# Opening in three sweeps, modulation loads one block later, six stage joints moved ahead, a candidates' search without copies, experts opened by quarters

## The chip, the core and the metric

The kernel runs on one core of one Trainium2 chip. The metric is device time in microseconds (us) of one execution; three runs give a median. The core's engines run side by side and wait for one another through semaphores: PE (TensorE, matmuls into the banks of `ps`), ACT (ScalarE), DVE (VectorE), and SP (SyncE), which here only issues DMAs, all of them on one queue in the order of the program.

## What is computed

Two transformer blocks on 256 tokens of width 2048. Cut to what the change touches:

```python
h = rms_norm(x, ln_gain); z = h @ w_in + b_in              # first projection: 77 blocks of 128 columns
y_a, y_b, y_c = recurrent(z), sparse_attention(z), decayed_attention(z)   # with silu gates
merged = sum(sigmoid(z_merge[j]) * (y_j @ w_branch[j]) for j in range(3))
h = x + merged @ w_out
h = h + sigmoid(h @ w_ple_gate) * rms_norm(p @ w_ple, ple_gain)
mod = silu(c) @ w_mod + b_mod                              # 96 blocks of modulation rows, on VectorE
h1, hc = modulate(h), modulate(ctx)                        # tokens and context, 256 rows each
# second mixer: projections of both (y), of the tokens alone (l), two branches, merge, w_out
q = modulate(h2) @ peer_w_q
s = einsum(q, sub_keys)                                    # 32 rows of 128 scores per token
top_s, top_i = top_k(s, 16)                                # "top"
best = top_k(top_s[0] + top_s[1], 16); wts = softmax(best) # "cand"
weights[expert, t] = wts spread over the 128 x 128 experts # "expw"
y = (weights * gelu(u @ h2)) .T @ v                        # 16384 experts, in 32 groups of 512
out = rmsnorm(h2 + g2 * y)
```

## The kernel before

Everything is transposed: a tile holds 128 channels by 256 tokens, 16 such tiles make one activation (`DC = 16`, `T = 256`). A weight block is 1 MB (128 columns of 2048 rows) or 0.5 MB, loaded into one of four slots of `ring` (`SLOTS = 4`); the load into a slot waits on SP until `weights_used` says that the block four before has been multiplied. Most products are made in three parts to keep precision: ACT rounds the weights (`round_z`, `round_block`, `round_branch`, ...), DVE subtracts to get the remainder (`split_z`, `split_block`, ...), and PE makes rounded x rounded, rounded x remainder and remainder x rounded, 48 matmuls for a 1 MB block (`three_products`, `split_products`). Rounding runs two blocks ahead of PE. The three engines' programs are written out by hand, stage behind stage; each engine executes its own strictly in order, so the order of calls in `n1_act`, `n1_dve`, `merge_act`, `out_act`, `experts_act` and so on sets what waits for what. ACT takes a finished block out of its bank with `keep_gate` or a copy.

Places that the change and the prediction speak of, in order of the program:

- **Opening** (`n1_*`). SP loads x in four quarters, then `consts` (848 KB) and `params` (294 KB), the first block of w_z, `cond` (2 MB), `misc`, `p`, and the first blocks of w_mod between those of w_z. ACT squares x; PE sums the squares with a matrix of ones from `consts` (16 float32 matmuls, L856); ACT takes the root, DVE inverts it and scales x by it; ACT rounds quarter after quarter (`r0` to `r3`, L832), DVE makes their remainders (`l0` to `l3`), and PE starts the first block when `l0` is there.
- **Modulation chunks** (`mod_chunk`, L760 and L763): 52 of the 96 are made by DVE inside the first projection's loop, ahead of the split of the block two further on; a chunk is one or two multiplications with accumulation over 2048 columns. `load_mod` on SP waits until the chunk two before is used.
- **Six joints** between stages, in which the next stage's first weights are rounded and split only after the last block of the stage before has been taken out: gates to branch products (`merge_*`), branch products to the ple product and w_out (`out_*`), ple gate to y (`n2_*`), y to l, second gates to second branch products (`merge2_*`), and those to the second w_out (`round_last`, `split_last`).
- **Candidates** (`choose_*`). DVE makes eight rounds of `top`, each of four score rows, then four rounds of `cand`; ACT makes the exponentials of a round of `cand`. Meanwhile PE multiplies the first four expert groups (`early`, 64 matmuls a group), and ACT applies the gelu to each. PE then needs `cand` and all four gelus to transpose the mixing weights (`mix`).
- **Expert weights** (`expw_*`): 64 rounds in a loop; for each DVE makes one block-diagonal tile (L3319) and two one-hot tiles (L3323), PE spreads them, ACT copies them out.
- **Experts** (`experts_*`): ACT rounds the normed activation in quarters, DVE makes remainders, then both go over the first 16 pieces of u; DVE clears the sum `yacc` (L3589), and the v phases begin.

## Time and profile before

| | |
|---|---|
| median of three runs | 4459.39 us (4456.03 to 4464.69) |
| the profiled execution's own time | 4466.13 us |
| its span, first to last instruction | 4464.4 us |
| mean granted clock of TensorE | 0.972 |
| data moved by DMA | 764.42 MB, mean 171 GB/s |
| PE, DVE, ACT busy | 95%, 67%, 45% of the span |

A row of a timeline gives the start and length in us of an instruction (or of several alike, xN), and in brackets how long its engine had been idle before it and what ended that. A granted clock of 1.0 stands for 2.4 GHz, 0.5 for 1.2 GHz.

### The profile page before, as it was taken

The page shows a single profiled execution, that of the slowest core. Times are in us where ns is not written, and L with a number is a line of the kernel's source. Part 1 is how long each engine was busy: PE and PEld are TensorE (multiplying, and loading weights), DVE is VectorE, ACT ScalarE, POOL GpSimd, SP SyncE. Part 2 cuts the span into 40 slices and gives each one's busy share as a digit, 9 for nine tenths or more (in the row PEclk, how much of TensorE's full clock was granted, in tenths as well). Part 3 has the DMA queues.
Part 4 walks back from the last instruction along what each step waited for, and adds up shares of the span by engine and source line. Part 5 has one row for each costly group of instructions (what it writes and reads, how often), then busy time and mean ns, then how long its engine had stood idle before and what let it go on. Part 6 is the DMA issues. An engine that isn't in the chain of part 4 may idle for free.

```text
span 4464.4 us, 66743 instructions
## 1 busy us (share of the span) xinstructions
PE 4220.8 (95%) x27552; PEld 3763.9 (84%) x27552; DVE 3004.3 (67%) x4776; ACT 2016.0 (45%) x3194; POOL 0.2 (0%) x4
## 2 busy tenths in 40 slices
PE   7999889999999989979998999988999999999998
PEld 7999868998988886778886999988788888888886
DVE  7887754666767664457776554687776767666666
ACT  4444464444452242444443434156455555555554
POOL 0000000000000000000000000000000000000000
PEclk9999999999999999989998999999999999999999
DMA  7888533367755442200002554424555454555552
GB/s 283 319 314 309 176 129 129 123 230 272 276 186 189 171 151 78 99 22 1 1 1 76 162 205 153 172 95 203 212 195 220 185 216 190 211 195 206 200 201 95
DMA packets 136927, 764.42 MB, mean 171 GB/s; under 512 B 12352, under 2 KB 30016, under 8 KB 67392
## 3 DMA queue, kind: packets, MB, share of 16 engines
q1 hardware_dynamic: 136640, 760.32, 46.5%
q8 instruction: 213, 3.49, 0.3%
q14 instruction: 74, 0.61, 0.0%
HBM read 737.20 MB, written 23.07 MB: 170 GB/s over the span
## 4 chain that ended last, share of the span: by engine, by line
PE 70%; DVE 9%; ACT 3%; DMA 2%; issue 1%; DVEq 0%; SPq 0%; ACTq 0%
PE ps L3450 15%; PE ps L3421 9%; PE ps L917 6%; PE ps L919 6%; PE ps L918 6%; PE ps L3423 5%; PE ps L2789 1%; PE ps L3349 1%; PE ps L2792 1%; PE ps L846 1%; PE ps L3341 1%; PE ps L847 1%; PE ps L848 1%; PE ps L2780 1%; DMA ring<-w_branch_dram 1%
## 5 line engine op out<-in xcount | busy, mean ns | idle before, releaser
L3450 PE MATMUL ps<-pieces,gact_parts 128*128 128x512 f32 x3072 | 710.5, 392 | 13.5 <-DVE pieces L3545 7.7
L3450 PEld LDWEIGHTS ps<-pieces,gact_parts 128*128 128x128 f32 x3072 | 578.9, 189 | 137.4 <-issue 6.6
L3421 PE MATMUL ps<-hp_parts,pieces 128*128 128x512 f32 x1792 | 635.6, 399 | 7.7 <-DVE pieces L3545 7.7
L848 PE MATMUL ps<-x_rounded,ring_rounded 128*128 128x256 f32 x2000 | 563.3, 282 | 0.0
L3545 DVE TENSOR_TENSOR pieces<-ring,pieces 128x512 fp32r<-128x512 f32 x464 | 320.8, 692 | 272.8 <-ACT pieces L3488 272.4
L3423 PE MATMUL ps<-hp_parts,pieces 128*128 128x256 f32 x1792 | 503.8, 281 | 0.0
L3488 ACT ACTIVATE pieces<-ring 128x512 fp32r<-128x512 f32 x464 | 293.0, 632 | 354.6 <-PE ps L3423 265.2
L3488 ACT ACTIVATE pieces<-area 128x512 fp32r<-128x512 f32 x496 | 311.6, 630 | 312.3 <-PE ps L3450 201.5
L3545 DVE TENSOR_TENSOR pieces<-area,pieces 128x512 fp32r<-128x512 f32 x496 | 341.4, 690 | 160.6 <-ACT pieces L3488 152.2
L3421 PEld LDWEIGHTS ps<-hp_parts,pieces 128*128 128x128 f32 x1792 | 337.6, 188 | 91.6 <-issue 7.9
L848 PEld LDWEIGHTS ps<-x_rounded,ring_rounded 128*128 128x128 f32 x2000 | 379.9, 190 | 0.0
L846 PE MATMUL ps<-x_rounded,z_rounded 128*128 128x256 f32 x1232 | 347.7, 282 | 17.2 <-DVE ring_rounded L814 10.4
L847 PE MATMUL ps<-hn_rest,z_rounded 128*128 128x256 f32 x1232 | 346.9, 282 | 0.0
L3423 PEld LDWEIGHTS ps<-hp_parts,pieces 128*128 128x128 f32 x1792 | 339.3, 189 | 1.1
L909 DVE TENSOR_TENSOR ring_rounded<-ring,ring_rounded 128x1024 fp32r<-128x1024 f32 x168 | 197.9, 1222 | 198.9 <-ACT ring_rounded L904 198.9
L919 PE MATMUL ps<-x_rounded,ring_rounded 128*128 128x256 f32 x1088 | 310.2, 285 | 0.0
L917 PE MATMUL ps<-x_rounded,ring_rounded 128*128 128x256 f32 x832 | 245.0, 294 | 21.9 <-DVE ring_rounded L909 21.9
L846 PEld LDWEIGHTS ps<-x_rounded,z_rounded 128*128 128x128 f32 x1232 | 233.2, 189 | 18.3 <-DVE ring_rounded L814 10.0
L846 PE MATMUL ps<-x_rounded,ring_rounded 128*128 128x256 f32 x768 | 224.0, 292 | 19.8 <-DVE ring_rounded L1008 19.5
L918 PE MATMUL ps<-hcat_rest,ring_rounded 128*128 128x256 f32 x832 | 238.7, 287 | 0.0
L814 DVE TENSOR_TENSOR ring_rounded<-ring,z_rounded 128x1024 fp32r<-128x1024 f32 x154 | 181.6, 1222 | 77.9 <-ACT z_rounded L808 77.6
L847 PEld LDWEIGHTS ps<-hn_rest,z_rounded 128*128 128x128 f32 x1232 | 233.3, 189 | 0.0
(538 smaller groups left out, 9425.7 us busy)
## 6 DMA issues: line engine op xcount, KB each, us to landing
ring<-u_dram SPq DMA_DIRECT2D x128, 1024.0 KB, 6.4
area<-v_dram SPq DMA_DIRECT2D x124, 1024.0 KB, 8.9
ring<-w_mod_dram SPq DMA_DIRECT2D x96, 1024.0 KB, 7.0
ring<-w_mg_dram SPq DMA_DIRECT2D x80, 1024.0 KB, 4.9
ring<-w_z_dram SPq DMA_DIRECT2D x77, 1024.0 KB, 6.9
ring<-w_branch_dram SPq DMA_DIRECT2D x80, 512.0 KB, 4.2
ring<-w_out_dram SPq DMA_DIRECT2D x32, 1024.0 KB, 5.0
ring<-w_y_dram SPq DMA_DIRECT2D x20, 1024.0 KB, 4.8
```

Source lines behind the costliest of these rows:

```text
L846: nc.tensor.matmul(out, rounded, hn_rounded[:, k, :], start=first, stop=False)
L847: nc.tensor.matmul(out, rounded, hn_rest[:, k, :], start=False, stop=False)
L848: return nc.tensor.matmul(out, rest, hn_rounded[:, k, :], start=False, stop=last)
L909: nc.vector.tensor_tensor(rest_piece(at, q), raw_piece(at, q), buffer(piece + q).bitcast(F32), ALU.subtract).then_inc(weights_split, 1)
L917: nc.tensor.matmul(out, w, rounded, start=(k == 0), stop=False)
L918: nc.tensor.matmul(out, w, rest, start=False, stop=False)
L919: return nc.tensor.matmul(out, w_rest, rounded, start=False, stop=(k == DC - 1))
L3421: both = nc.tensor.matmul(bank(s).rearrange("p (a t) -> p a t", t=T), piece[:, b, 0, k * P:(k + 1) * P], hp2[:, :, c, :], start=(c == 0), ...
L3423: last = nc.tensor.matmul(bank(s, 0, T), piece[:, b, 1, k * P:(k + 1) * P], hp2[:, 0, c, :], start=False, stop=(c == DC - 1))
L3450: last = nc.tensor.matmul(out, gact[:, k, ga, s, t * P:(t + 1) * P], piece[:, b, va, :], start=(s == 0 and w == 0), stop=(s == GROUP - 1 a ...
L3488: nc.scalar.activation(piece[:, n % NPIECES, 0, :], source, ACT.Copy).then_inc(rounded, 1)
L3545: nc.vector.tensor_tensor(piece[:, b, 1, :], source, piece[:, b, 0, :].bitcast(F32), ALU.subtract).then_inc(remainders, 1)
```

## The change

1. The opening: the ones are made in the kernel by a memset, pairs of squares are added on DVE so that PE sums 8 matmuls instead of 16, ACT loads the root's table first, and the first three blocks are multiplied in three sweeps: rounded by rounded for all three, then rounded by the activation's remainder, then the weights' remainder by rounded. `consts`, `misc`, `p` and the first two modulation blocks are loaded behind the fourth block.
2. Modulation chunks begin at block 4 instead of 0 (52 chunks over 73 blocks), each loaded one block later in SP's order.
3. The six joints: the first block of the next stage is rounded (and at three of them split) ahead of the last take-out; the ple product's copies run before the rounding of w_out; the first y block multiplies its context half first.
4. `top` reads the scores and writes values in place, without row and value copies or memsets, in eight written-out rounds.
5. The first four rounds' one-hot tiles are made before the wait for `mix`; experts' quarters are rounded, split and multiplied one by one; the clearing of `yacc` is gone, its first addition is a copy.

```diff
+MODS_FROM = 4
+MODS_AT = {MODS_FROM + n * (77 - MODS_FROM) // (77 - MERGE_MODS): n for n in range(77 - MERGE_MODS)}
 MOD_ORDER = [2 * DC + n // 7 * 2 + n % 7 // 3 - 1 if n % 7 in (3, 6) else n // 7 * 5 + n % 7 - n % 7 // 3 for n in range(42)]
...
+            norm.wait("dve", "cell")
+            norm("table", nc.scalar.activation(table_cell, table_cell, ACT.Sqrt))
...
-            round_z(act, 0)
+                norm(f"squares{q}", nc.scalar.activation(sq[:, v, :], xc[:, v, :], ACT.Square))
+            act.wait_ge(params_landed, 16)
...
+            round_z(act, 0)
...
+                if q == 0:
+                    round_z(act, 1)
+            do.end()
+            round_z(act, 2)
...
+                do.wait("dve", f"pairs{q}")
+                for c in range(4 * q, 4 * q + 2):
+                    last = nc.tensor.matmul(bank(4, 0, T), first_ones, sq[:, c, :], start=(c == 0), stop=(c == DC - 3))
...
+            for q in range(4):
+                for k in range(4 * q, 4 * q + 4):
+                    whole(0, k, True)
+            for b in (1, 2):
+                for k in range(DC):
+                    whole(b, k, False)
+            for q in range(4):
+                S["hn_split"].upto(pe, "dve", f"l{q}", 0)
+                for b in range(Z_FIRST):
+                    for k in range(4 * q, 4 * q + 4):
+                        nc.tensor.matmul(bank(b, 0, T), piece_of(b, k), hn_rest[:, k, :], start=False, stop=False)
+            for b in range(Z_FIRST):
+                for k in range(DC):
+                    q, c = divmod(k, 8)
+                    if c == 0:
+                        pe.wait_ge(weights_split, 2 * b + q + 1)
+                    last = nc.tensor.matmul(bank(b, 0, T), rest_piece(b, q)[:, c * P:(c + 1) * P], hn_rounded[:, k, :], start=False, stop=(k == DC - 1))
+                last.then_inc(weights_used, 1)
...
-                elif b == 1:
-                    pe.wait_ge(inputs_loaded, N_INPUTS * 16)
...
+            norm("cell", nc.vector.memset(table_cell, 1.0))
+            norm("ones", nc.vector.memset(first_ones, 1.0))
+            for q in range(4):
+                norm.wait("act", f"squares{q}")
+                norm(f"pairs{q}", nc.vector.tensor_tensor(sq[:, 4 * q:4 * q + 2, :], sq[:, 4 * q:4 * q + 2, :], sq[:, 4 * q + 2:4 * q + 4, :], ALU.add))
+            dve.wait_ge(params_landed, 16)
...
+            for b in range(Z_FIRST):
                 split_z(dve, b)
-            pre_dve(dve)
...
+                if b == Z_AHEAD:
+                    pre_dve(dve)
...
-            act.wait_ge(weights_used, last_at(b - 2) + 1)
...
+                if i == N_GATES - 1:
+                    round_branch(act, 0)
...
         def out_act(act):
-            round_run(act, 0)
...
-                    round_run(act, 1)
+                round_run(act, idx)
             norm = Do(act, st_e, "act")
...
+                if j == N_Y - 1:
+                    round_l(act, 0)
...
+                    for k in range(DC):
+                        split_products(pe, out[:, 1, :], streams["y"].first, Y_PIECES, run_buffer, k, hcat_rounded[:, 1, k, :], hcat_rest[:, 1, k, :])
                     S["norm2"].upto(pe, "act", "root", 0)
                 for k in range(DC):
                     if j == 0:
                         S["hcat_split"].upto(pe, "dve", f"l{k}", 0)
-                    last = split_products(pe, bank(j % SLOTS).rearrange("p (s t) -> p s t", s=2), streams["y"].first + j, Y_PIECES + 2 * j, run_buffer, k,
-                                          hcat_rounded[:, :, k, :], hcat_rest[:, :, k, :])
+                        last = split_products(pe, out[:, 0, :], streams["y"].first, Y_PIECES, run_buffer, k, hcat_rounded[:, 0, k, :], hcat_rest[:, 0, k, :])
+                    else:
...
+            split_l(dve, 0)
...
+                if i == N_GATES2 - 1:
+                    round_branch2(act, 0)
...
                 if dc:
                     merged2_remainder(dc - 1)
...
+                row = [r * LANES + l for l in each_lane]
                 for l in each_lane:
-                    do(f"row{l}", nc.vector.tensor_copy(krow[:, l, :], scores[:, r * LANES + l, :]))
-                gate(0)
+                    do(f"m0_{l}", nc.vector.max(topv[:, row[l], 0:8], scores[:, row[l], :]))
...
-                gate(1)
+                    do(f"rest{l}", nc.vector.match_replace(krest[:, l, :], topv[:, row[l], 0:8], scores[:, row[l], :], -BIG))
...
+                    do(f"i0_{l}", nc.vector.max_index(kidx[:, l, 0:8], topv[:, row[l], 0:8], scores[:, row[l], :]))
+                do.own()
                 for l in each_lane:
-                    do(f"rest{l}", nc.vector.match_replace(krest[:, l, :], kval[:, l, 0:8], krow[:, l, :], -BIG))
-                gate(2)
+                    do(f"m1_{l}", nc.vector.max(topv[:, row[l], 8:16], krest[:, l, :]))
...
+                    do(f"i1_{l}", nc.vector.max_index(kidx[:, l, 8:16], topv[:, row[l], 8:16], krest[:, l, :]))
+                do.own()
+                do("indices", nc.vector.tensor_copy(topi[:, row[0]:row[0] + LANES, :], kidx))
...
         def expw_dve(dve):
+            dve.wait_ge(peer_loaded, 16)
+            S["mix"].upto(dve, "act", "idx", 0)
+
+            def hot_rows(r, u):
+                for k, hot in enumerate(hots[u][1:]):
+                    last = nc.vector.tensor_tensor(hot, iota[:, None, :].to_broadcast([P, NB4, P]),
+                                                   idxt[:, k, bass.ds(r * NB4, NB4)].rearrange("p (t o) -> p t o", o=1).to_broadcast([P, NB4, P]), ALU.is_equal)
+                return last
+
+            for u in range(4):
+                hot_rows(u, u).then_inc(first_hot_made, 1)
...
-                    bd, hot1, hot2 = hots[u]
+                    bd = hots[u][0]
                     if later(r, 4):
...
+                                                start=(j == 0 and k == 0), stop=False)
                         last = nc.tensor.matmul(bank(s, 0, T), piece[:, b, 1, k * P:(k + 1) * P], hp2[:, 0, c, :],
-                                                start=False, stop=(c == DC - 1))
+                                                start=False, stop=(j == 3 and k == 3))
                     last.then_inc(pieces_used, 1)
...
                 if q == 0:
                     act.wait_ge(tail_stored, 16)
                 do(f"r{q}", nc.scalar.activation(hp2[:, 0, 4 * q:4 * q + 4, :], hp[:, 4 * q:4 * q + 4, :], ACT.Copy))
-            do.end()
-            u_act(act, EARLY, 0)
+                round_piece(act, n, n, u_source(n))
+            do.end()
+            u_act(act, EARLY, 0, 4)
             round_gact(act, 0, 0)
...
-                last = nc.vector.tensor_tensor(y, y, bank(4 + 2 * (dc % 2) + t), ALU.add)
+                y, made = yacc[:, t, dc * PIECE:(dc + 1) * PIECE], bank(4 + 2 * (dc % 2) + t)
...
             do = Do(dve, st_hps, "dve")
-            for q in (1, 2, 3, 0):
+            for n, q in enumerate(QUARTERS):
                 do.wait("act", f"r{q}")
                 v = slice(4 * q, 4 * q + 4)
                 do(f"l{q}", nc.vector.tensor_tensor(hp2[:, 1, v, :], hp[:, v, :], hp2[:, 0, v, :].bitcast(F32), ALU.subtract))
-            do.end()
-            for n in range(PER_PHASE):
                 remainder(dve, n, n, u_source(n))
-            dve.wait_ge(w_stored[0], 32)
-            nc.vector.memset(yacc, 0.0).then_inc(zeroed, 1)
+            do.end()
...
+                remainder(dve, n, n, u_source(n))
             weigh(dve, 0, 0)
             split_gact(dve, 0, 0)
-            dve.wait_ge(zeroed, 1)
...
-            for dst, src in ((consts[:, :], a["consts"]), (params[:, :], a["params"])):
...
+                        if b == Z_FIRST - 1:
                             sp.dma_start(silu1, a["cond"].rearrange("p (c n) -> p c n", c=2)).then_inc(cond_loaded, 16)
+                        if b == Z_FIRST:
+                            sp.dma_start(consts[:, :], a["consts"]).then_inc(norm_inputs, 16)
+                            for n in range(2):
+                                load_mod(sp, n, n)
                             sp.dma_start(misc[:, :], a["misc"]).then_inc(inputs_loaded, 16)
                             sp.dma_start(pT, a["p"].rearrange("p (k t) -> p k t", t=T)).then_inc(inputs_loaded, 16)
-                        if b in MODS_AT:
-                            load_mod(sp, MODS_AT[b], MODS_AT[b])
+                        if MODS_AT.get(b - 1, 0) >= 2:
+                            load_mod(sp, MODS_AT[b - 1], MODS_AT[b - 1])
                     sp.dma_start(lru_w, a["w_lru"].rearrange("c p n -> p c n")).then_inc(lru_landed, 16)
                     continue
```

How the instructions stand on two engines, as rows of each engine's program with the semaphores that they wait on.

VectorE at its start, in the opening, of the kernel before:

```order
L814 TENSOR_TENSOR ring_rounded<-ring,z_rounded 128x1024 [waits weights_rounded,norm_inputs_landed]
L814 TENSOR_TENSOR ring_rounded<-ring,z_rounded 128x1024 [waits weights_rounded]
L879 RECIPROCAL area<-area 128x256 [waits norm_x_act_steps]
L883 SCALAR_TENSOR_TENSOR area<-x,params,area 128x256 [waits norm_x_dve_steps]
L883 SCALAR_TENSOR_TENSOR area<-x,params,area 128x256 x7
L887 TENSOR_TENSOR hn_rest<-area,x_rounded 128x1024 [waits hn_split_act_steps]
```

and of the changed one:

```order
L908 MEMSET area 128x1
L909 MEMSET area 128x128
L912 TENSOR_TENSOR area<-area 128x512 [waits norm_x_act_steps] x4
L915 RECIPROCAL area<-area 128x256 [waits norm_x_act_steps,params_landed]
L918 SCALAR_TENSOR_TENSOR area<-x,params,area 128x256 [waits norm_x_dve_steps]
L918 SCALAR_TENSOR_TENSOR area<-x,params,area 128x256 x15
L923 TENSOR_TENSOR hn_rest<-area,x_rounded 128x1024 [waits hn_split_act_steps] x4
L815 TENSOR_TENSOR ring_rounded<-ring,z_rounded 128x1024 [waits weights_rounded] x10
L785 TENSOR_SCALAR halves<-params 128x64 [waits norm_inputs_landed,inputs_loaded]
```

The split of the first weights has moved behind all of the activation's scaling and remainders, and five blocks are split before the first wait for the late inputs.

VectorE in the candidates' search, one round of `top` (`area` holds scores, values and indices), before:

```order
L3220 COPY area<-area 128x128 x3
L3217 MEMSET area 128x1 [waits top_dve_steps]
L3223 MAX area<-area 128x8 x4
L3217 MEMSET area 128x1 [waits top_dve_steps]
L3226 MAX_INDEX area<-area 128x8 x4
L3228 MATCH_REPLACE area<-area 128x128 x4
L3217 MEMSET area 128x1 [waits top_dve_steps]
L3231 MAX area<-area 128x8 x4
L3217 MEMSET area 128x1 [waits top_dve_steps]
L3234 MAX_INDEX area<-area 128x8 x4
L3236 COPY area<-area 128x16 x4
L3239 CAST area<-area 128x16 [waits top_dve_steps]
```

and of the changed one:

```order
L3266 MATCH_REPLACE area<-area 128x128 [waits top_dve_steps]
L3266 MATCH_REPLACE area<-area 128x128 x3
L3268 MAX_INDEX area<-area 128x8 x4
L3271 MAX area<-area 128x8 [waits top_dve_steps]
L3271 MAX area<-area 128x8 x3
L3274 MAX_INDEX area<-area 128x8 [waits top_dve_steps]
L3274 MAX_INDEX area<-area 128x8 x3
L3276 CAST area<-area 128x64 [waits top_dve_steps]
```

The copies and memsets are gone and four casts have become one; the searches themselves are as many as before.

VectorE at the experts' opening, before:

```order
L3584 TENSOR_TENSOR hp_parts<-area,hp_parts 128x1024 [waits hn_split_act_steps,weights_kept]
L3584 TENSOR_TENSOR hp_parts<-area,hp_parts 128x1024 [waits hn_split_act_steps] x3
L3545 TENSOR_TENSOR pieces<-ring,pieces 128x512 [waits pieces_rounded] x16
L3589 MEMSET area 128x4096 [waits expert_weights_stored_0]
L3559 TENSOR_TENSOR x<-x,ring 128x4x4x64 [waits early_groups_kept,expert_weights_landed_0]
```

and of the changed one:

```order
L3637 TENSOR_TENSOR hp_parts<-area,hp_parts 128x1024 [waits hn_split_act_steps,weights_kept]
L3598 TENSOR_TENSOR pieces<-ring,pieces 128x512 [waits pieces_rounded]
L3637 TENSOR_TENSOR hp_parts<-area,hp_parts 128x1024 [waits hn_split_act_steps]
...
L3598 TENSOR_TENSOR pieces<-ring,pieces 128x512 [waits pieces_rounded] x13
L3612 TENSOR_TENSOR x<-x,ring 128x4x4x64 [waits early_groups_kept,expert_weights_landed_0]
```

A piece of u now follows each quarter of the activation, and the memset between the last piece and the first weighing is gone.

## Rows read from the trace of the kernel before

**Rows 1.** Page, part 1: busy us (share of span) xinstructions per engine.

```profile
PE 4220.8 (95%) x27552; PEld 3763.9 (84%) x27552; DVE 3004.3 (67%) x4776; ACT 2016.0 (45%) x3194; POOL 0.2 (0%) x4
```

**Rows 2.** Timeline, opening: start us, us, instructions, [idle before <-releaser].

```profile
8.54 1.06 ACT L823 ACTIVATE area<-x 128x1024 f32<-128x1024 f32 x1 [0.26 <-DMA x<-x_dram]
...
11.41 9.54 PE L856 MATMUL ps<-area,consts 128*128 128x256 f32 x32 [11.41 <-DMA params<-params_dram]
...
20.98 0.47 ACT L827 ACTIVATE area<-ps,params 128x256 f32<-128x256 f32 x1 [3.81 <-PE ps L856]
...
24.98 1.06 ACT L832 ACTIVATE x_rounded<-area 128x1024 fp32r<-128x1024 f32 x1 [3.53 <-DVE area L883]
...
27.72 0.58 PE L846 MATMUL ps<-x_rounded,z_rounded 128*128 128x256 f32 x1 [6.78 <-DVE hn_rest L887]
...
50.10 0.58 PE L846 MATMUL ps<-x_rounded,z_rounded 128*128 128x256 f32 x1 [8.13 <-DVE ring_rounded L814]
```

**Rows 3.** Timeline of the first projection: DVE early on, ACT at its end.

```profile
60.07 2.29 DVE L760 SCALAR_TENSOR_TENSOR ps<-ring,area 128x2048 f32<-128x2048 f32 x1
...
64.49 2.36 DVE L814 TENSOR_TENSOR ring_rounded<-ring,z_rounded 128x1024 fp32r<-128x1024 f32 x2
...
473.18 0.47 ACT L842 ACTIVATE area<-ps,params 128x256 f32<-128x256 f32 x1 [5.18 <-PE ps L848]
...
478.83 0.47 ACT L842 ACTIVATE area<-ps,params 128x256 f32<-128x256 f32 x1 [5.18 <-PE ps L848]
```

**Rows 4.** Timeline, PE: first matmul behind each of six joints.

```profile
930.71 0.36 PE L1613 MATMUL ps<-branch_in,ring_rounded 128*128 128x256 f32 x1 [2.96 <-DVE ring_rounded L968]
...
1090.74 9.16 PE L1726 MATMUL ps<-p,ring 128*128 128x256 f32 x32 [5.42 <-ACT area L1784]
...
1312.96 0.77 PE L917 MATMUL ps<-hcat_rounded,y_rounded 128*128 128x512 f32 x1 [4.73 <-DVE hcat_rest L1914]
...
1541.26 0.35 PE L917 MATMUL ps<-x_rounded,ring_rounded 128*128 128x256 f32 x1 [3.08 <-DVE ring_rounded L909]
...
2516.39 0.36 PE L2984 MATMUL ps<-branch_in,ring_rounded 128*128 128x256 f32 x1 [2.87 <-DVE ring_rounded L955]
...
2613.10 0.55 PE L917 MATMUL ps<-hcat_rest,ring_rounded 128*128 128x256 f32 x1 [5.33 <-DVE ring_rounded L909]
```

**Rows 5.** Timeline, ACT and DVE at the second, third and sixth joint.

```profile
1087.69 2.00 ACT L904 ACTIVATE y_rounded<-ring 128x1024 fp32r<-128x1024 f32 x2 [7.44 <-DMA ring<-w_out_dram]
...
1323.97 0.49 DVE L1914 SCALAR_TENSOR_TENSOR hcat_rest<-area,mod,hcat_rounded 128x256 fp32r<-128x256 f32 x1 [0.18 <-ACT hcat_rounded L1832]
...
2609.05 2.00 ACT L904 ACTIVATE ring_rounded<-ring 128x1024 fp32r<-128x1024 f32 x2 [7.10 <-DMA ring<-w_out_dram]
```

**Rows 6.** Windows: us, busy us per engine, granted clock, DMA share, GB/s.

```profile
2721.00:2724.00 3.00, 3.00 (x11) 2.30 (x12) 2.59 (x8) 2.83 (x8) 0.00 (x0) 0.50 0.01 3
```

**Rows 7.** Timeline of the candidates' search, DVE, ACT and PE.

```profile
2828.92 0.63 DVE L3220 COPY area<-area 128x128 f32<-128x128 f32 x4 [16.25 <-ACT area L3119]
...
2888.90 1.43 DVE L3249 TENSOR_TENSOR area<-area 128x256 f32<-128x256 f32 x4 [0.21 <-DVE area L3239]
...
2938.73 1.02 ACT L3128 ACTIVATE x<-ps 128x1024 f32<-128x1024 f32 x1 [0.50 <-PE ps L3174]
...
2944.83 1.09 PE L3182 MATMUL ps<-consts,area 128*128 128x128 f32 x4 [6.14 <-DVE area L3288]
```

**Rows 8.** Timeline around the expert weights' first group, DVE and PE.

```profile
2954.11 0.69 DVE L3319 TENSOR_TENSOR area<-area 128x512 f32<-128x512 f32 x1 [9.43 <-ACT area L3144]
...
2956.16 1.19 PE L3341 MATMUL ps<-area 128*128 128x128 f32 x4 [5.53 <-DVE area L3323]
```

**Rows 9.** Timeline of the experts' opening, PE and DVE.

```profile
3087.53 0.77 PE L3421 MATMUL ps<-hp_parts,pieces 128*128 128x512 f32 x1 [7.73 <-DVE pieces L3545]
...
3108.49 3.47 DVE L3589 MEMSET area<- 128x4096 f32 x1 [0.80 <-issue]
...
3116.14 2.47 PE L3450 MATMUL ps<-pieces,gact_parts 128*128 128x512 f32 x5 [4.29 <-DVE pieces L3545]
```

146 lines of the change are left out of this document (69 added, 77 removed).

## The prediction

> **What bounds the kernel now.** I read the page first: PE is busy 95% of the span [rows 1], and no other engine comes near. So the time is PE's work, which the change leaves almost untouched, plus the places where PE stands still or runs at its lower clock. I therefore went through the timeline of PE for every idle time over 1 us and kept those that the change touches: three waits in the opening [rows 2], six joints [rows 4], the wait for the candidates [rows 7], that for the first group of expert weights [rows 8] and two at the experts' opening [rows 9]. Summed, they are some 75 us. The reader is to see in each row who ended the wait, since what is late next decides how much of it comes back. Behind each joint the loads are issued as slots come free, so later stages shift with PE and keep what was gained. All times below are on the axis of the profiled execution.
>
> **Opening, -18 us.** Before: the ones are in `consts`, so PE waits for two small loads until 11.41, sums for 9.54 us (0.6 us a matmul), the root starts at 20.98, the first rounded quarter is there at 26.04, 5.06 us after the root's start, and PE begins at 27.72 [rows 2]. It stops again for 8.13 us before the third block, because DVE made two modulation chunks ahead of the third block's split [rows 2]. The last block is taken out at 478.83, and a block takes 478.83 - 473.18 = 5.65 us [rows 3].
>
> After: the last squares end at 9.6 [rows 2]; a pair addition of 512 columns is half of a 1024-column subtraction (1.2 us, half of 2.36 for two [rows 3]), 0.6 us, so PE has the last pair at 10.4 and two matmuls end at 11.6 or, at the lower clock, 12. Root at 12.1, first rounded quarter 5.06 us later, at 17.2: PE begins there, 10.5 us sooner. It does not run through. The sweep over block 0 follows ACT's quarters, between which one weight block is rounded (2 us), to about 23. Blocks 1 and 2 take 16 matmuls each; a matmul costs 5.65/48 = 0.118 us, twice that at half clock, which I give to block 0 and 1: 3.4 and 1.9 us, to 28.4. The second sweep, 48 matmuls, ends at 34.0, the third at 39.7. DVE is ahead of both: 16 scalings to 21, four remainders of 1.2 us to 26, six splits to 33. From 39.7, 74 blocks of 5.65 are 418.1 us. DVE is late once more: its late chore (cond_silu, 4096 columns, twice a chunk's 2.2 us, behind the fifth block's split at 45, then the sixth's split) puts chunk 0 at 52, and a block with a double chunk costs it 2 x 2.2 + 2.3 = 6.7 us [rows 3] against PE's 5.65; three in a row make PE wait about 1 us each. 39.7 + 418.1 + 3.0 = 460.8 against 478.8. Bounds: 21 us with no stall and the full clock throughout; 12 us if block 2's work comes late by 3 us and each of the first six chunks, not three, costs 1 us. Rather than by DVE, a chunk could be late by its load, now two blocks (11.3 us) ahead of its use instead of three; that is a rival below.
>
> **Joints.** *Gates to branches, -2.0:* the wait is 2.96 us [rows 4]. The first branch block is rounded and split before the last gate is out, so it goes; but DVE still does the second split and silu3 (2.3 us) before it can take the first product out and split the third block, which comes about 1 us late. Bounds 1 to 3. *Ple product, -7.0:* ACT waited 7.44 us for w_out and only then copied the ple product [rows 5]; PE waited 5.42 us [rows 4] and then ran 32 matmuls in 9.16 us [rows 4]; without the pause I reckon 7.1, the 2 us being what the lower clock behind a pause costs elsewhere (below, y). The copies now come first; w_out is there at 1087.7 as before, its split is ready at 1091, and PE is through the ple product at 1092.5 instead of 1099.5. The second w_out block is rounded at 1095.5, wanted at 1098. Bounds 5 to 7.5. *Y, +1.0:* the 4.73 us of waiting [rows 4] are filled with the context half (48 x 0.118 = 5.65 us), but the token half needs all 16 remainders, and the last is made at 1324.46 as before [rows 5]. PE ended this block at about 1326.1 (1312.96, 48 matmuls of double width, 11.3 us, and 1.9 for the cold start). So at most 0.5 us can come back. Against it stands the clock: the token half is now 3 x 0.118 = 0.35 us of work every 0.8 us. Where the trace has such a stretch, PE fed by remainders one at a time, the granted clock stays at 0.50 for all of it [rows 6], and the following block begins at half clock, which costs 1.9 us for the first 3.7 us of it. From -0.5 to +1.5 I take +1.0, as that row is the nearest.
>
> By the Trainium skill ("TensorE: Matmul & The Clock Gate", section "HAM oscillation — how this bites in real kernels") waits between short bursts of matmuls throttle the engine, so that each burst starts cold. By that rule the y joint loses its 1.5 us, and the first sweep stays slow as well; by a clock that holds, the joint would gain 0.5 us, and the whole sum would be 1.5 us better than mine.
>
> *Y to l, -3.0:* 3.08 us [rows 4]; the modulation and the weights that it needs are there some us earlier, the first split is done in time and the second needs 4 us of PE's 5.65. *Second gates to branches, -2.8:* 2.87 us [rows 4], the same pattern without silu3. *Second w_out, -1.7:* 5.33 us [rows 4], but ACT gets these weights only at 2609.05 [rows 5], so the split's first half is ready at 2611.3, not before 2607.8; 2613.1 - 2611.35 comes back. The last branch take-out now queues behind that split on DVE, until 2612.8; its remainder is the 16th that PE asks for, so it is in time. Bounds 0 to 3.
>
> **Candidates, -4.9.** Eight rounds of `top` take DVE from 2828.92 to 2888.90, 7.5 us each [rows 7]. Four row copies (0.63 us [rows 7]), four memsets with their waits, value copies, three casts and the loop's own instructions go, about 2 us a round, 16 in all. It does not come through whole. PE makes its four early groups between 2828.9 and 2938.7, 27.5 us each, so the second is there at 2884, and ACT's second gelu (1.0 us [rows 7]), a table load and the four exponentials (3 us together, an estimate) stand ahead of DVE's masking, which it could begin at 2882. It waits until about 2887.6; so 11 us of the 16 are left, and DVE would end at 2934. PE, however, is busy with its early groups until 2938.7, and the fourth gelu ends at 2939.75 [rows 7]: nothing starts before. PE's start moves from 2944.83 to 2939.9. Bounds 3 to 5. Of the 16 us that leave DVE two thirds are hidden.
>
> **Expert weights, -1.2.** DVE makes three tiles (0.69 us and 1.29 for two) before PE can start at 2956.16 [rows 8]; now only the first is left behind `mix`, the eight one-hot tiles having been made in the 9.43 us in which DVE waited. 1.2 us; up to 3 if DVE's lead of eight tiles (5 us) also speeds the loop, which I doubt since it waits for PE from the fifth round on.
>
> **Experts' opening, -7.4.** PE waited 7.73 us for four roundings, four remainders and a piece [rows 9]. Now one of each: rounding 1.0, then remainder 1.2 and piece 0.6 give PE a start at 3084.15 instead of 3087.53, 3.4 us. The next pieces follow every 1.9 us, PE at half clock needs 2.6 for each. Then the 4.29 us before the first v phase [rows 9]: 0.80 of idling and the 3.47 us of memset go; weighing, rounding and split (3.4 us) remain and nearly fit in PE's last pieces: 4.0. Bounds 5 to 8.
>
> **The sum:** 18.0 + 2.0 + 7.0 - 1.0 + 3.0 + 2.8 + 1.7 + 4.9 + 1.2 + 7.4 = 47.0 us. The profiled execution took 4466.1 us, 6.7 over the median; so 4419 on its axis and **4412 us** as a median.
>
> **Rivals.** *Part of it is given back* (chance 0.22): the opening only brings 12 (its lower bound), the ple joint 5, the w_out joint nothing, the candidates 3 and the experts 5: 47.0 - 6 - 2 - 1.7 - 1.9 - 2.4 = 33, 4426 us. For it speaks that in the opening five queues meet in 40 us; against it that each wait in the rows names one releaser, which is moved. *More than forecast* (0.12): the upper bounds of opening, expert weights, branches and y: 47 + 3 + 1.8 + 1 + 1.5 = 54, 4405 us. *The modulation becomes the bound, slower than before* (0.03): with 52 chunks over 73 blocks and loads one block later, a chunk whose load is late stops DVE, then the split behind it, then PE, in every block that has one. That decides from 47/52 = 0.9 us a chunk on; at 1.2 us it would be 4459 + 15 = 4474 us. Against it: DVE's mean load would be some 92% of the loop, and a load has 11.3 us. *The joints are hidden anyway* (0.02): if what is saved were taken back by DMA, whose loads for the next stage are not issued sooner than PE frees the slots, only opening and experts would stay: 25 us, 4434. Forecast itself: 0.61.
>
> **Range and chances.** Its own case spans 4407 to 4421; the partial rival reaches to 4430, the better one to 4403. I give 4403 to 4429, which leaves out 0.05 for the slower cases and 0.1 at the ends. All but the slower rival lie more than 0.2% (9 us) below 4459.4, about what three runs can tell from no change: faster 0.95, same 0.02, slower 0.03.
>
> **What would show it.** Right: z begins at about 17 us and its last block is out at 461; PE's idle times before the first branch, l and second branch products are gone; 32 ple matmuls in 7 us without a pause; after `top` DVE waits for ACT, and PE's wait before `mix` is about 1.1 us behind the last early group; no memset before the first weighing. Wrong: DVE waiting for w_mod loads in the z loop; the token half of y paced at clock 0.5 for long behind it; new idle times before the third branch block or the second w_out block of more than 1 us.

## The result, and the profile after

The changed kernel takes **4401.5 us** (median of 4 runs, 4396.87 to 4402.85) beside 4462.04 us of the kernel before (4 runs, 4456.03 to 4466.32): ratio **0.9864**, interval 0.9851 to 0.9877, so 60.5 us less. The forecast was 4412 us, between 4403 and 4429, and 47 us less. The direction and most of the places were right. The forecast gain was 22% too small, and the time lies 1.5 us below the range. The interval of the ratio allows gains of 55 to 66 us, so the 47 us are missed by more than noise, the lower end of the range not.

The page after (part 1; beside [rows 1]): PE is busy for 18.7 us less than before. The pair sums of the opening explain 3.5 of them (9.54 us in [rows 2], 6.01 now); the rest is a first sign that more went than idle time: other matmuls became shorter.

```profile
span 4400.4 us, 66555 instructions
...
PE 4202.1 (95%) x27584; PEld 3752.2 (85%) x27584; DVE 2991.4 (68%) x4661; ACT 2011.7 (46%) x3194; POOL 0.2 (0%) x4
```

PE's waits in the opening, and ACT's take-out of the last z block (timeline: start us, us, instruction, [idle before <- releaser]; beside [rows 2, 3]). PE begins with z at 17.95 (forecast 17.2), and the last block is out at 460.64 (forecast 460.8). The waits at 56.89 to 70.28 are the three short ones forecast, 0.61 to 0.80 us each where about 1 us was written. (The first is put down to ACT's take-out, which ended 0.1 us behind the first half of DVE's split.) For a modulation load DVE waits once in this stage, 1.2 us.

```profile
17.95 1.20 PE L873 MATMUL ps<-x_rounded,z_rounded 128*128 128x256 f32 x4 [5.38 <-ACT x_rounded L835]
20.70 7.41 PE L873 MATMUL ps<-x_rounded,z_rounded 128*128 128x256 f32 x44 [1.55 <-ACT x_rounded L835]
56.89 0.36 PE L850 MATMUL ps<-x_rounded,z_rounded 128*128 128x256 f32 x1 [0.61 <-ACT area L846]
63.59 0.36 PE L850 MATMUL ps<-x_rounded,z_rounded 128*128 128x256 f32 x1 [0.80 <-DVE ring_rounded L815]
70.28 0.36 PE L850 MATMUL ps<-x_rounded,z_rounded 128*128 128x256 f32 x1 [0.80 <-DVE ring_rounded L815]
...
460.64 0.47 ACT L846 ACTIVATE area<-ps,params 128x256 f32<-128x256 f32 x1 [5.18 <-PE ps L852]
```

PE's waits at the later places (same view, beside [rows 4], [rows 7], [rows 8] and [rows 9]). Four of the six joints have no wait over 0.3 us left and so no row. At y the token half is paced by remainders, with 0.17 us of waiting eleven times. The second w_out kept 3.81 of 5.33 us, the mix 1.11 of 6.14, the expert weights 5.25 of 5.53 and the experts' opening 4.33 of 7.73; the wait ahead of the first v phase is gone.

```profile
1286.10 0.38 PE L953 MATMUL ps<-hcat_rounded,y_rounded 128*128 128x256 f32 x1 [0.17 <-DVE hcat_rest L1951]
...
2568.82 0.55 PE L953 MATMUL ps<-hcat_rest,ring_rounded 128*128 128x256 f32 x1 [3.81 <-DVE ring_rounded L945]
...
2896.76 0.66 PE L3229 MATMUL ps<-consts,area 128*128 128x128 f32 x4 [1.11 <-ACT x L3175]
2906.16 3.45 PE L3389 MATMUL ps<-area 128*128 128x128 f32 x16 [5.25 <-DVE area L3367]
...
3032.38 0.77 PE L3473 MATMUL ps<-hp_parts,pieces 128*128 128x512 f32 x1 [4.33 <-DVE pieces L3598]
```

In the two profiled executions the lead of the changed kernel (by how much sooner it starts the same matmul) is 18.2 us when the z stage is left, 29.7 to 30.3 in the w_out stage, 34.8 in the first l blocks, 43.0 before the candidates, 51.6 in the experts' weights, 60.9 in the first v phase and 64.0 at the end. Idle time of PE makes 45.3 us of it (243.5 before, 198.2 after). The other 18.7 are PE's busy time: 3.5 us of pair sums, and 15 us of matmuls that ran shorter, as the time at clock 0.50 fell from 246 to 191 us. Not all of this happened where the change had been made. Between 1586 and 1721 us, in code that it leaves alone, the lead first fell by 3.3 and then rose by 6.4.

### The profile page after: what moved, and what is told of

Its sections match the earlier page's. It is cut to its first block, busy times and chain, and to the rows that moved or that the text cites. A ratio compares the mean times of both kernels' runs of the same rounds, so it can differ in the third digit from the quotient of the medians.

```text
span 4400.4 us, 66555 instructions
## 1 busy us (share of the span) xinstructions
PE 4202.1 (95%) x27584; PEld 3752.2 (85%) x27584; DVE 2991.4 (68%) x4661; ACT 2011.7 (46%) x3194; POOL 0.2 (0%) x4
## 4 chain that ended last, share of the span: by engine, by line
PE 73%; DVE 7%; ACT 3%; DMA 2%; issue 1%; SPq 0%; DVEq 0%; ACTq 0%
PE ps L3501 15%; PE ps L3473 10%; PE ps L953 6%; PE ps L954 5%; PE ps L955 5%; PE ps L3475 5%; PE ps L3221 3%; PE ps L2833 1%; PE ps L3397 1%; PE ps L2836 1%; PE ps L3389 1%; PE ps L850 1%; PE ps L851 1%; PE ps L852 1%; DVE ring_rounded L945 1%; PE ps L2824 1%
## 5 line engine op out<-in xcount | busy, mean ns | idle before, releaser
L852 PE MATMUL ps<-x_rounded,ring_rounded 128*128 128x256 f32 x1952 | 548.5, 281 | 0.0
L852 PEld LDWEIGHTS ps<-x_rounded,ring_rounded 128*128 128x128 f32 x1952 | 369.4, 189 | 0.0
L850 PE MATMUL ps<-x_rounded,z_rounded 128*128 128x256 f32 x1184 | 331.8, 280 | 2.2 <-DVE ring_rounded L815 1.6
L851 PE MATMUL ps<-hn_rest,z_rounded 128*128 128x256 f32 x1184 | 331.7, 280 | 0.0
L955 PE MATMUL ps<-x_rounded,ring_rounded 128*128 128x256 f32 x1088 | 310.5, 285 | 0.0
L953 PE MATMUL ps<-x_rounded,ring_rounded 128*128 128x256 f32 x832 | 245.2, 295 | 19.5 <-DVE ring_rounded L945 19.5
L850 PE MATMUL ps<-x_rounded,ring_rounded 128*128 128x256 f32 x768 | 224.6, 292 | 19.7 <-DVE ring_rounded L1044 19.4
L850 PEld LDWEIGHTS ps<-x_rounded,z_rounded 128*128 128x128 f32 x1184 | 222.2, 188 | 2.7 <-ACT area L846 1.8
L851 PEld LDWEIGHTS ps<-hn_rest,z_rounded 128*128 128x128 f32 x1184 | 222.2, 188 | 0.0
L851 PE MATMUL ps<-hn_rest,ring_rounded 128*128 128x256 f32 x768 | 218.0, 284 | 0.0
```

The lines of the kernel that those rows point to most:

```text
L850: nc.tensor.matmul(out, rounded, hn_rounded[:, k, :], start=first, stop=False)
L851: nc.tensor.matmul(out, rounded, hn_rest[:, k, :], start=False, stop=False)
L852: return nc.tensor.matmul(out, rest, hn_rounded[:, k, :], start=False, stop=last)
L953: nc.tensor.matmul(out, w, rounded, start=(k == 0), stop=False)
L955: return nc.tensor.matmul(out, w_rest, rounded, start=False, stop=(k == DC - 1))
```

## The experiments

**Is it the kernel or the execution?** Both kernels were run again, unchanged, and the changed one later a third time.

> The kernel before, unchanged, to see what one execution differs from another in. The change saved 64 us between the two profiled executions and 60.5 us between the medians, where I had summed 47. Of the 17 us in the profiles, 8 lie in stages that the change does not touch, where only the stretches at clock 0.5 fall differently (from 1586 to 1721 alone 3.2 us, 1957 to 1997 2.2 us, the last 50 us 3.0 us). Theory A (chance): these stretches fall anew in every execution; then the idle times here agree with those of the first profile within 0.1 us, but the time spent at clock 0.5 in the untouched stages differs by several us, and the stage from 1685.8 to 1721.2 (35.3 us) may take 29 to 35. Theory B (fixed): the same program always has its slow stretches in the same places; then every stage agrees within 0.5 us. Ratio to the kernel before 1.000 in either case.

> The changed kernel, unchanged, timed in five rounds. Both theories expect 0.986 to 0.987 of the kernel before. Theory A expects that the stages from 1551.8 to 1683.1 of its profile (131.4 us, 17 us of them at clock 0.5) take another time by 1 us or more; theory B that they agree within 0.5 us.

Measured: 1.0001 (0.9991 to 1.0010) and 0.9866 (0.9852 to 0.988). Theory B fell with the second profile of the changed kernel. Windows over the same instructions (busy us of PE, granted clock, DMA share, GB/s), from 1662.51 in the first profile of the changed kernel:

```profile
1662.51:1683.13 20.62, 18.96 (x104) 1.00 0.25 83
```

and in the second, from 1656.70:

```profile
1656.70:1683.76 27.06, 25.40 (x103) 0.75 0.19 64
```

The idle time is 1.66 us in both, and one took 6.4 us longer, with half of it at clock 0.50. Over the 14 profiles of this study this stage takes 28.9, 33.8 or 35.4 us (counted from 1685.8 of before), with the change or without it. So a single pair of profiles can't tell whom such a difference belongs to, and 8 of the 17 us by which the profiles' lead exceeds the forecast lie in stages that the change leaves alone. The medians, which average over executions, exceed it by 13.5 us. Waits, on the other hand, mostly agreed within 0.1 us.

> The changed kernel once more, beside the one with added products. Expected 0.9865 of the kernel before, and for the stage that took 20.6 and 27.1 us in the two profiles of it one of these two values again.

Measured: 0.9858 (0.9843 to 0.9874), and the longer of the two values (35.40).

**Do the parts add up?** Each of these is one part of the change applied alone, or all but one:

```text
 open_only:    before + MODS_FROM, pair sums, three sweeps, later constants and modulation loads
 no_open:      after  - the same
 joints_only:  before + the six joints
 experts_only: before + expert weights and experts' opening
```

> The kernel before with the three-sweep opening and the later modulation loads alone. Both theories expect the last z block's end 18.2 us earlier (about 460.8) and the same idle times behind it. If the lead is kept to the end, the time is 18 us less, ratio 0.996. A rival (C): the opening shifts every later stretch of clock 0.5 to better places, and so carries part of the unexplained 13.5 us; then the ratio is 0.994 or less.

> The changed kernel with the opening and the modulation loads as before. If parts add up, 60.5 - 18 = 42 us less than before, ratio 0.9905; rival C expects less than 38 us, ratio over 0.9915. My prediction's own terms without the opening sum to 29 us (0.9935): the theory that I priced each joint's pause right and the rest is chance expects that value.

> The kernel before with the six stage joints moved ahead, and nothing else. My prediction's terms for them sum to 15.5 us (0.9965); between the two profiled executions they gave 19.6 us (2.5 + 8.6 + 0.2 + 4.9 + 2.2 + 1.3), which theory D explains by the slow stretches behind the removed waits and expects again, ratio 0.9956. If it is 15.5 or less, the excess of the result was chance or lies elsewhere.

> The kernel before with the experts' weights and the experts' opening changed, and nothing else. My terms sum to 8.6 us (0.9981); the profiled executions showed 12.9 us (1.9 + 1.6 + 3.6 + 4.4 + 1.4), of which 7.8 us are idle time and the rest a clock that stays at 1.00. Theory D expects 11 to 13 us (0.9972), the reading by idle times alone 8 to 9 us.

Measured, as ratios to the kernel before: 0.9958 (0.9945 to 0.9971), 0.9908 (0.9895 to 0.9921), 0.9945 (0.9926 to 0.9964) and 0.9972 (0.9959 to 0.9984), that is 18.8, 41, 24.6 and 12.5 us (by the medians alone 20.1, 42.3, 29.2 and 16.5, which shows how far such values can be trusted). The opening brings what was forecast and nothing later: rival C falls. Theory D in these texts says that a removed wait takes along the stretch at half clock behind it. The joints' 24.6 us exclude my 15.5 (0.9965, just outside the interval); the experts' 12.5 lie where theory D had them, though my 8.6 is still inside that interval. The profiles of these kernels allow more: the time between the same two matmuls, averaged over all profiles without and with a part (number of profiles in brackets, us).

| term | forecast | without | with | measured |
|---|---|---|---|---|
| opening | 18.0 | 483.3 (5) | 464.8 (4) | 18.5 |
| gates to branches | 2.0 | 221.5 (4) | 217.6 (7) | 3.9 |
| ple product | 7.0 | 108.9 (4) | 102.0 (7) | 6.9 |
| y | -1.0 | 33.6 (4) | 33.5 (7) | 0.1 |
| y to l | 3.0 | 246.5 (4) | 241.7 (7) | 4.9 |
| second gates to branches | 2.8 | 142.0 (4) | 138.3 (7) | 3.7 |
| second w_out | 1.7 | 84.8 (4) | 83.7 (7) | 1.2 |
| candidates | 4.9 | 44.7 (5) | 39.7 (6) | 5.0 |
| expert weights | 1.2 | 33.5 (4) | 31.2 (6) | 2.2 |
| experts' opening | 7.4 | 161.8 (4) | 151.7 (7) | 10.1 |
| sum | 47.0 | | | 56.5 |

y to l is the clearest row: the four durations without it lie within 0.02 us of each other, and so do the seven with it. 3.2 of the 4.9 us are the wait; 1.6 are the 10 us behind it, of which 3.4 had been at clock 0.50 and none is now. Windows of 10 us from the first l matmul, before and after:

```profile
1541.26:1551.26 10.00, 10.00 (x72) 0.83 0.25 78
...
1508.03:1518.03 10.00, 10.00 (x86) 1.00 0.59 208
```

Two rows have to be read with care. The line between "gates to branches" and "ple product" lies inside the branch products (at 1033.03 of before). From the ple product's own first matmul (1078.26 of before) the second row gives 8.0 us, and the first, up to there, 2.9.

And at the second gates to branches the clock has next to no part. The wait of 2.87 us is there in four profiles; in three of them the clock stays at 1.00 behind it, and in one it falls for 3.4 us, which costs 1.3 us. The kernel before, in its first profile and in the second:

```profile
2516.39:2524.39 8.00, 8.00 (x67) 1.00 0.34 96
...
2517.53:2525.53 8.00, 8.00 (x56) 0.81 0.21 69
```

So this joint gave 3.3 us at once. The other 0.4 built up evenly over the next 80 us, and such a difference in pace also stands between executions of one kernel: the same 504 matmuls take 59.1 us in the changed kernel's first profile and 59.8 in its third.

**What does a wait cost beside its own length?** Ten waits are put into the steady z loop, where the clock of the changed kernel is otherwise at 1.00: TensorE waits for a memset on GpSimd that starts when the block before is through.

```diff
+                if b in PAUSES:
+                    pe.wait_ge(paused, list(PAUSES).index(b) + 1)
...
+            for n, (b, count) in enumerate(PAUSES.items()):
+                pool.wait_ge(weights_used, b)
+                if n:
+                    pool.wait_ge(paused, n)
+                nc.gpsimd.memset(cut(ZAT + (N_Z - 10) * T, count), 0.0).then_inc(paused, 1)
```

> The changed kernel with ten added pauses of TensorE in the steady loop over the z blocks, before blocks 10, 16, 22 and so on to 64: TensorE waits for one memset on GpSimd of 500, 1000, 1500, 2000 or 2500 columns, twice each. The question is what a pause costs beside its own length. Theory D (a pause of more than about 2.5 us brings on a stretch at clock 0.5, and where the pause goes, that goes too, which I priced at nothing in four of the joints): pauses under 2 us cost their length and 0.1 us at most, those over 3 us their length and another 1.7 to 3.4 us. The rival (B2: the stretches at clock 0.5 have another cause, as many transfers or DVE's accesses, and a pause costs its length): every pause costs its length and under 0.4 us, with the clock at 1.00 behind it.

Measured (timeline, then windows of 6 us from the first matmul behind the waits of 1.93 and 2.35 us, columns as above):

```profile
188.67 0.36 PE L850 MATMUL ps<-x_rounded,z_rounded 128*128 128x256 f32 x1 [1.93 <-issue]
225.18 0.55 PE L850 MATMUL ps<-x_rounded,z_rounded 128*128 128x256 f32 x1 [2.35 <-issue]
```

```profile
188.67:194.67 6.00, 6.00 (x51) 1.00 0.79 322
225.18:231.18 6.00, 6.00 (x39) 0.75 0.74 307
368.41:374.41 6.00, 6.00 (x51) 1.00 0.79 328
404.92:410.92 6.00, 6.00 (x38) 0.72 0.30 124
```

The eight waits of 0.68 to 1.93 us left the clock alone. Both waits of 2.35 us had 3.4 us at 0.50 beside them; the 6 us behind them hold 39 and 38 matmuls, not 51, and they took 1.4 and 1.5 us more than the trend of the shorter ones leads to (two blocks last 12.65, 13.07 and 13.48 us around 1.10, 1.51 and 1.93, and 15.25 and 15.42 around 2.35). Longer ones, with a twin of each that is filled with products nobody reads:

```diff
+                if b in FILLED:
+                    for n in range(FILLED[b]):
+                        nc.tensor.matmul(bank(b % SLOTS, 0, T), hn_rounded[:, 0, 0:P], hn_rounded[:, 0, :], start=True, stop=True)
```

> As the run with ten pauses, with longer ones: one memset of 2500 columns, two of 1700, two of 2300, three of 2000, three of 2500 (waits of about 2.4, 3.2, 4.1, 5.3 and 6.5 us), before blocks 10 to 34 as they are, and the same five again before blocks 40 to 64, each filled with 16, 22, 30, 40 and 50 products that nobody reads. In the first run the four waits of up to 1.93 us at either end of the row had the clock at 1.00 behind them, and both waits of 2.35 us were followed by 3.4 us at 0.50, which made the stretch 1.3 to 1.4 us longer than its neighbours' trend. Theory D: all five unfilled waits have 3.4 to 7 us at 0.50 behind them and cost 1.3 to 3.4 us more than the filled ones, longer waits no less; the five filled ones have the clock at 1.00. Rival B2: filled and unfilled cost the same.

Windows of 6 us behind the unfilled waits of 2.34, 3.25, 4.25, 5.57 and 6.82 us, then behind three of their filled twins:

```profile
82.64:88.64 6.00, 6.00 (x51) 1.00 0.75 302
120.06:126.06 6.00, 6.00 (x29) 0.53 0.58 236
161.00:167.00 6.00, 6.00 (x29) 0.53 0.02 5
203.27:209.27 6.00, 6.00 (x34) 0.64 0.20 81
246.20:252.20 6.00, 6.00 (x29) 0.52 0.01 2
...
322.70:328.70 6.00, 6.00 (x50) 1.00 0.66 232
361.13:367.13 6.00, 6.00 (x51) 1.00 0.42 171
441.85:447.85 6.00, 6.00 (x50) 1.00 0.01 3
```

From the start of the block before the wait to the start of the second one behind it, unfilled against filled took 17.34 against 14.80 us, 18.34 against 15.80, 19.06 against 17.12 and 20.99 against 18.39: **2.5, 2.5, 1.9 and 2.6 us** beside the wait itself, and 0.0 for the wait of 2.34 us this time. B2 falls: the memset is the same for both twins, and the price goes with the clock. It does not grow with the wait.

**Does it hold at the kernel's own waits?** The changed kernel with such products in eight waits that are left; here the one ahead of l blocks 11, 15 and 19:

```diff
                 pe.wait_ge(evacuated, evacuated_from["l"] + j - SLOTS + 1)
+                idle_products(bank(j % SLOTS, 0, T), hn_rounded[:, 0, :], {11: 30, 15: 46, 19: 14}.get(j, 0))
```

> The changed kernel with products that nobody reads in eight of the waits that are left: before the first gate block (4.8 us), before the second path's gate blocks 16 and 17 (3.0 and 3.0), before l blocks 11, 15 and 19 (4.3, 6.3, 2.3), before the first block of the second w_out (3.8) and of peer_q (4.9). They fill 60 to 90% of each wait and end before it does; nothing else moves, so the idle time is gone without a gain of its own. Theory D: the clock stays at 1.00 behind the filled waits, which gives 1 to 2 us at each of the seven blocks and 5 us or more at peer_q's first block, whose 13.5 us at clock 0.5 follow a wait of 4.9 us: 10 to 20 us in all, ratio 0.982 to 0.984 of the kernel before. Rival B2: no change, 0.986 to 0.987, or slower by up to 3 us where the added products end late.

Measured: 0.9865 (0.9845 to 0.9884), no gain. The expected gain did not come. Behind the first gate block and the three l blocks 1.4, 2.0, 1.9 and 0.7 us were won, against the mean of the three profiles of the changed kernel (against its first profile alone the l blocks seem to have won 2 us more, as they took longest in that one). Ahead of gate block 16, w_out and peer_q the products themselves ended 1.9, 1.5 and 2.5 us late, because they began at the half clock, stood behind a wait that they should have stood ahead of, or were float32 on both sides (0.43 us for one, 0.12 for one of the rounded kind). And 0.9 of the first gate block's 1.4 us were lost again 90 us later, where nothing had been changed: ahead of the q and k norm is a wait with a slow stretch behind it, and with the earlier start more of that stretch falls on matmuls. Windows of 7 us from the norm's first matmul, without the products (the changed kernel) and with them:

```profile
556.82:563.82 7.00, 7.00 (x32) 0.72 0.01 2
...
554.61:561.61 7.00, 7.00 (x25) 0.58 0.02 7
```

The lateness mended, with seven waits and none before peer_q:

```diff
-                    idle_products(bank(6 + i % 2, 0, T), hn_rounded[:, 0, :], 20)
+                    idle_products(bank(6 + i % 2, 0, T), hn_rounded[:, 0, :], 11)
...
+            idle_products(bank(4, 0, T), branch2_in[:, 0, 0, :], 26)
```

> The kernel with added products again, mended where they ended late: in the first version they cost 1.9 us before gate block 16, 1.5 us before w_out and 2.5 us before peer_q, and it won 1.4, 2.7, 2.4 and 1.5 us at the first gate block and the three l blocks. Now 11 products, not 20, before gate blocks 16 and 17, those before w_out ahead of all its waits, none before peer_q. Theory D: 1.4 + 2.7 + 2.4 + 1.5, 1 to 2 at w_out and 1 at the gate blocks, 10 us in all, so 0.984 of the kernel before and 0.9977 of the changed kernel. Rival E: what is won at one place is lost at others, because the slow stretches merely fall elsewhere, and the time is that of the changed kernel within 3 us.

Measured: **4392.26 us** (5 runs, 4391.24 to 4400.93), ratio 0.9840 (0.9827 to 0.9854), beside 4402.66 us of the changed kernel timed next to it: 10.4 us by the medians, 8 us by the ratios. By its ratio it is the fastest kernel of the study, but its interval still overlaps that of the changed kernel (0.9843 to 0.9874), so the size of the gain is not settled. Windows over l blocks 11 and 15 with the waits ahead of them, first without the products:

```profile
1578.00:1600.00 22.00, 17.68 (x117) 0.84 0.35 122
1610.00:1630.00 20.00, 13.71 (x97) 0.83 0.34 113
```

and with them:

```profile
1575.00:1594.00 19.00, 18.59 (x147) 1.00 0.34 120
1602.00:1622.00 20.00, 19.56 (x160) 1.00 0.33 109
```

Last, four more waits (before the q and k norm, the transposes, the expert weights and the experts' opening, so eleven in all):

> The kernel with added products, now in ten waits: those of the six-block version (its seven waits less none) and four more, before the norm of the first q and k channels (5.6 us, 40 products), before the transposes behind it (6.0, 44), before the experts' weights (5.3, 16 products with four passes each) and before the experts' opening (4.3, 15 of these). Theory D: the seven known waits give 10 us against the changed kernel, as measured; the four new ones 1.3 to 2.5 us each less what ends late, 3 to 8 us more: 0.9825 to 0.9835 of the kernel before. Rival E: what is won falls elsewhere, 0.984 or more.

Measured: 4394.44 us, 0.9841 (0.9827 to 0.9854), nothing more. In the profile the first new place won 2.2 us and the second 1.1 to 1.6. The other two gave 0.0 and -0.5, as their float32 products ended 1.5 and 1.8 us late. The branches and the first w_out stage, where the kernels are alike, took some 4 us more than in the changed kernel's first profile. Rival E's time came out. Its reason, that what is won is lost elsewhere, is shown at the q and k norm; how much of these 4 us is of that kind is not shown.

## Why the prediction was wrong

**The step that failed** is the reading at its start: "PE's work, which the change leaves almost untouched, plus the places where PE stands still or runs at its lower clock", from which I then summed the idle times alone. The rows of the joints name a wait's length and its releaser; what follows the wait stands in the granted clock, and I counted it at one joint only (ple, 2 us, measured 2.0 right behind the wait) and put it at nothing elsewhere. At y to l I wrote the wait's 3.0 us; 4.9 came, 1.6 of them from the clock. At the first gates to branches I wrote 2.0; 4.9 came at once, 1.8 of them behind the wait, which was followed by 3.4 us at clock 0.50, and the next branches took 1.0 back in waits of PE. At the experts' opening 3.4 of idle time were right (3.5 measured), but behind the wait ahead of v the first 24 us took 2.1 us less, for which I had nothing, and the pieces up to it 4.6 where I had 4.0. The expert weights brought 2.2 instead of 1.2: the candidates' wait of 6.14 us, now 1.11, had slowed the matmuls of the mix behind it. Windows from the first matmul of the mix to the first of the weights, before and after:

```profile
2944.83:2956.16 11.33, 5.79 (x37) 0.80 0.00 0
...
2896.76:2906.16 9.40, 4.15 (x36) 0.98 0.28 104
```

With the experts' part alone, which leaves the candidates' wait in place, this stretch gave 1.1 us, with both 1.9. At the second gates to branches (2.8 forecast, 3.7 measured) the clock brought only 0.3. In all, some 6 of the 9.5 us between forecast and table are slow stretches behind removed waits, and 1.1 are the sign of y. The waits put into the z loop gave the price in isolation: 1.9 to 2.6 us beside any wait of 3.25 to 6.82 us.

**Y had the wrong sign.** I took +1.0 us, since [rows 6] show the clock at 0.50 where PE is fed remainder by remainder. Here it was not:

```profile
1283.95:1296.00 12.05, 9.48 (x51) 1.00 0.30 122
```

PE is busy 79% of these 12 us and the clock stays at 1.00 throughout. PE came to them straight from the context half. Ahead of the stretch of [rows 6] stands a wait of 4.9 us, which I had not weighed: I had taken the nearest row by its pace alone. With products in that wait the same block began at the full clock, which then fell all the same, for 10.2 us instead of 20.5:

```profile
2674.30:2680.00 5.70, 4.50 (x30) 1.00 0.00 1
2680.20:2690.40 10.20, 9.90 (x39) 0.50 0.28 89
```

So the wait accounts for about half of it. Why the pace brings the clock down there, and does not at y, is open. The rule that I weighed there, from the Trainium skill's page "TensorE: Matmul & The Clock Gate", section "HAM oscillation — how this bites in real kernels", is of waits between bursts; the trace agrees for the waits of 3.25 us and more above, and not for y's token half, whose waits are 0.17 us each. The clock held, and the joint gained 0.1 us where by a held clock I had worked out 0.5. The same page's section "Why this matters for your kernels" advises against long idle times between bursts of matmuls; the runs here agree, with the price above for each.

**The candidates** came out as worked out: a round of `top` takes 5.45 us instead of 7.5, 16 us go, and PE gains 5.0. DVE waits 5.55 us for ACT's exponentials, which begin behind the second gelu and a table load of 1.28 us, and the mix starts behind the fourth gelu and not behind DVE.

```profile
2840.43 1.02 ACT L3175 ACTIVATE x<-ps 128x1024 f32<-128x1024 f32 x1 [26.60 <-PE ps L3221]
2841.47 1.28 ACT L3183 ACT_TABLE_LOAD   x1
...
2844.51 1.43 DVE L3312 TENSOR_TENSOR area<-area 128x256 f32<-128x256 f32 x4 [5.55 <-ACT area L3183]
```

**Right as well:** the opening (18.5 for 18.0) and w_out with 1.2 for 1.7. The ple product came out in the table (6.9 for 7.0) partly by luck: from its own first matmul it gave 8.0, and the branches before it took 1.0 back. Its mechanism was right: w_out came to ACT behind the first two of its copies, and PE did not stop. The three-in-a-hundred rival, modulation as the bound, did not come about.

**The axis.** The median of three runs that I started from, 4459.4 us, was low: timed again four times, the kernel before has medians of 4465.6, 4466.7, 4464.8 and 4463.8 us (17, 13, 9 and 9 runs). This does not touch the forecast gain, but it moved the forecast time down by some 5 us and so hid part of the error: single executions of this one kernel reach from 4454.8 to 4472.8.

**What stays open.** The terms add up to 56.5 us and the medians give 60.5. Executions of one kernel differ by more than this rest, and it was not traced to a place. What decides between 28.9 and 35.4 us in the stage of 1685.8, with at most 1.1 us of waiting ahead of any instruction, was not found either, nor why a wait of 2.87 us lowered the clock in one execution and not in three.

## What to carry to other kernels

Price a removed wait of the matrix engine as its idle time plus the slow stretch behind it, read from the granted clock or, where the trace allows, from the same instructions elsewhere at full clock. Before calling a difference between two profiles a gain, profile the same kernel twice. Where a wait of some 3 us can't be removed, products without a reader can fill it, if they stand ahead of the wait and end well before it does, at half clock too; here that brought 1.4 to 2.0 us at three places, 0.7 at a fourth, and 8 to 10 us in all on overlapping intervals. What is won ahead of another wait can be lost in the slow stretch behind that one.

## What was not expected of the hardware

- Waits of 0.68 to 1.93 us left TensorE's clock at its upper level in eight of eight cases; one of 2.35 us brought it to the lower in two of three; four of four from 3.25 us on did, for 6.8 to 10.2 us, at a price of 1.9 to 2.6 us that does not grow with the wait. Of the kernel's own waits one of 2.87 us lowered it in one of four profiles, one of 3.08 us in four of four.
- TensorE held the full clock for 12 us at 79% busy, with eleven waits of 0.17 us in them.
- One stage of 104 matmuls takes 20.6 or 27.1 us in two executions of the same program with the same 1.66 us of idle time. The whole time at clock 0.50 is 190.7, 197.0 and 207.9 us in three executions of one kernel. The Trainium skill ("TensorE: Matmul & The Clock Gate", section "What's actually happening") calls the number of slow matmuls at a kernel's start "run-variable"; here the same holds for the stretches in its middle.
